# Two attention stages: weighing on GpSimd, the second head's copies on VectorE, scores as three f32r products

## The reference

```python
ss = jnp.einsum('qghd,gqkd->gqhk', qi, k_sel).astype(jnp.float32) * scale
smask = (k_pos <= t[None, :, None])[:, :, None, :]
p_s = jax.nn.softmax(jnp.where(smask, ss, NEG), axis=-1)
o_s = jnp.einsum('gqhk,gqkd->qghd', p_s.astype(dt), v_sel)
...
o = gi[..., 0:1] * o_c + gi[..., 1:2] * o_s + gi[..., 2:3] * o_w
```

## Time and profile before

| | us |
|---|---|
| median of 3 runs | 2058.59 |
| the profiled execution | 2057.08 |
| its span | 2055.2 |
| TensorE busy | 2026.5 |
| VectorE busy | 1181.4 |
| ScalarE busy | 796.5 |
| GpSimd busy | 27.0 |

### The profile page before, as it was taken

The page is one execution under the profiler, slowest core; times in us unless marked ns, Lnnn a source line. Parts: engine busy times, 40 slices in busy tenths (PEclk is TensorE's granted clock), DMA queues, the critical chain, the costliest instruction groups (busy, mean ns, idle before and its releaser), DMA issues.

```text
span 2055.2 us, 25553 instructions
## 1 busy us (share of the span) xinstructions
PE 2026.5 (99%) x9922; PEld 1647.7 (80%) x9922; DVE 1181.4 (57%) x1801; ACT 796.5 (39%) x1297; POOL 27.0 (1%) x58
## 2 busy tenths in 40 slices
PE   9999999999999999999999999999999999999998
PEld 8865878888888888877888888878886588888886
DVE  6777645454445356556565764764525857476475
ACT  4258242332212223245542432443324844243343
POOL 1000000000000000000000000000000000000000
PEclk9999999999999999999999999999999999999999
DMA  7310412322222222321323222231322132322222
GB/s 252 108 42 20 140 36 103 113 91 95 101 103 82 102 103 73 122 87 58 113 73 113 85 100 102 97 118 52 114 103 92 42 113 73 112 102 83 101 102 72
DMA packets 39425, 194.87 MB, mean 95 GB/s; under 512 B 4744, under 2 KB 13096, under 8 KB 19840
## 3 DMA queue, kind: packets, MB, share of 16 engines
q1 hardware_dynamic: 36240, 183.34, 25.3%
q0 software_dynamic: 2880, 9.88, 1.7%
q10 hardware_dynamic: 208, 0.33, 0.1%
HBM read 188.83 MB, written 2.15 MB: 93 GB/s over the span
## 4 chain that ended last, share of the span: by engine, by line
PE 93%; DVE 3%; ACT 2%; DVEq 1%; DMA 1%; issue 1%; SPq 0%; ACTq 0%
PE bank L443 26%; PE bank L444 26%; PE bank L445 26%; PE bank L1514 2%; PE bank L1501 2%; PE bank L1482 1%; PE bank L529 1%; PE bank L530 1%; PE bank L534 1%; DVE w_lo L391 1%; PE bank L2509 1%; ACT w_hi L372 1%; PE bank L2501 1%; PE bank L1707 0%; ACT work L1581 0%
## 5 line engine op out<-in xcount | busy, mean ns | idle before, releaser
L372 ACT ACTIVATE w_hi<-w_raw 128x2048 fp32r<-128x2048 f32 (+3 forms) x165 | 302.2, 1832 | 721.6 <-PE bank L445 679.0
L443 PE MATMUL bank<-a_hi,w_hi 128*128 128x512 f32 (+1 forms) x1408 | 540.6, 384 | 0.0
L445 PE MATMUL bank<-a_hi,w_lo 128*128 128x512 f32 (+1 forms) x1408 | 537.8, 382 | 0.0
L444 PE MATMUL bank<-a_lo,w_hi 128*128 128x512 f32 (+1 forms) x1408 | 537.8, 382 | 0.0
L391 DVE TENSOR_TENSOR w_lo<-w_raw,w_hi 128x2048 fp32r<-128x2048 f32 (+3 forms) x163 | 358.6, 2201 | 254.7 <-ACT w_hi L372 254.7
L445 PEld LDWEIGHTS bank<-a_hi,w_lo 128*128 128x128 f32 x1408 | 264.7, 188 | 51.7
L443 PEld LDWEIGHTS bank<-a_hi,w_hi 128*128 128x128 f32 x1408 | 264.8, 188 | 51.3 <-issue 0.8
L444 PEld LDWEIGHTS bank<-a_lo,w_hi 128*128 128x128 f32 x1408 | 264.8, 188 | 50.0
L443 PE MATMUL bank<-w_hi,big_halves 128*128 128x512 f32 x384 | 150.2, 391 | 0.3 <-DVE w_lo L391 0.3
L445 PE MATMUL bank<-w_hi,big_halves 128*128 128x512 f32 x384 | 149.5, 389 | 0.0
L444 PE MATMUL bank<-w_lo,big_halves 128*128 128x512 f32 x384 | 149.4, 389 | 0.0
(11 more groups left out here) (384 smaller groups left out, 2556.9 us busy)
## 6 DMA issues: line engine op xcount, KB each, us to landing
w_raw<-in_w_fu SPq DMA_DIRECT2D x44, 1024.0 KB, 4.8
w_raw<-in_w_up SPq DMA_DIRECT2D x16, 1024.0 KB, 4.8
w_raw<-in_w_down SPq DMA_DIRECT2D x16, 1024.0 KB, 4.8
w_raw<-in_w_fd SPq DMA_DIRECT2D x16, 1024.0 KB, 4.8
w_raw<-in_w_fd SPq DMA_DIRECT2D x8, 768.0 KB, 4.2
w_raw<-in_w_rqk SPq DMA_DIRECT2D x4, 1024.0 KB, 5.3
w_raw<-in_w_rvg SPq DMA_DIRECT2D x4, 1024.0 KB, 5.0
w_raw<-in_w_gate SPq DMA_DIRECT2D x4, 1024.0 KB, 4.8
```

Of the source, the lines that this page charges most:

```text
L372: act.activation(dst[0][:, cols], raw[slot][:, cols], ACT.Copy).then_inc(hi_half_ready.sem if half == 0 else hi_ready.sem, 1)
L443: pe.matmul(out, w[0], x[0], start=first, stop=False)
L444: pe.matmul(out, w[0], x[1], start=False, stop=False)
L445: return pe.matmul(out, w[1], x[0], start=False, stop=last)
```

## The change

GpSimd gets the tensor-scalars of `weigh`. VectorE keeps the reciprocal (`invert`) and gets the copies of the second head's turned tiles; ScalarE keeps the first head's. VectorE's step becomes maximum(s), invert(s-1), copy(s-3), take, and in the second attention `stage_low` for the next pair in steps of kind 0. TensorE waits for each head's copy on a semaphore of its own.

The scores become three f32r products. For this the queries and keys are staged as a high half (a ScalarE copy) and a low half (a VectorE subtraction). In the first attention six tiles are staged once, from the dense stage before, behind `outputs_copied` (L1816); in the second two tiles for each pair. The bias rows of the second attention are issued between GpSimd's weighings.

```diff
@@ tensor: score(u)
-                    if u == 0:
-                        pe.wait_ge(*ready)
+                    if u % G == 0:
+                        pe.wait_ge(staged.sem, b_st + staged_for(n))
...
-                    for i, w, at in members(u):
-                        for e in range(2):
-                            last = pe.matmul(out[e][:, at:at + w], q[heads[e], i * P:(i + 1) * P], k[heads[e], 0:w],
-                                             start=at == 0, stop=not causal and (i, at) == GROUPS[u % G][-1])
+                    for a, b in ((0, 0), (0, 1), (1, 0)):
+                        for i, w, at in members(u):
+                            for e in range(2):
+                                last = pe.matmul(out[e][:, at:at + w], q[a][heads[e], i * P:(i + 1) * P], k[b][heads[e], 0:w],
+                                                 start=a == 0 and b == 0 and at == 0,
+                                                 stop=not causal and a == 1 and (i, at) == GROUPS[u % G][-1])
@@ tensor: turn(u)
                     for e in range(2):
                         if u >= 1:
-                            pe.wait_ge(probs_copied.sem, b_c + 2 * u + e - 1)
+                            pe.wait_ge(copied[e][0], copied[e][1] + u)
@@ vector
+            def stage_low(dve, n):
+                for r, (st, src) in enumerate(stagings(n)):
+                    dve.wait_ge(high_staged.sem, b_hi + once + n * each + r + 1)
+                    dve.tensor_tensor(st[1], src, st[0].bitcast(F32), ALU.subtract).then_inc(staged.sem, 1)
...
-                def weigh(u):
-                    n, count = u // G, 2 * len(members(u))
+                def invert(u):
+                    count = 2 * len(members(u))
                     dve.wait_ge(probs_ready.sem, b_p + parts_until(u + 1))
-                    dve.reciprocal(row_sum[u % 3][:, 0:count], row_sum[u % 3][:, 0:count])
-                    dve.drain()
-                    for r, (i, w, at) in enumerate(members(u)):
-                        for e in range(2):
...
+                    dve.reciprocal(row_sum[u % 3][:, 0:count], row_sum[u % 3][:, 0:count]).then_inc(sums_inverted.sem, 1)
+
+                def copy(u):
+                    n, p = u // G, u // G % 2
+                    if n >= 2:
+                        dve.wait_ge(out_ready.sem, b_o + n - 1)
+                    dve.wait_ge(probs_turned.sem, b_t + 2 * u + 2)
+                    for i, w, at in members(u):
+                        if i == 3:
+                            dve.tensor_copy(turned_keys(p, 1, 3), turn_bank[1][:, 3 * P:4 * P])
+                        m = min(i + 1, 3)
+                        last = dve.tensor_copy(probs_t[p][1][:, 0:m, i * P:(i + 1) * P],
+                                               turn_bank[1][:, at:at + m * P].rearrange("p (j t) -> p j t", t=P))
+                    last.then_inc(second_copied.sem, 1)
@@ vector: step(s)
                     if unit(1) is not None:
-                        weigh(unit(1))
+                        invert(unit(1))
+                    if unit(LAG) is not None:
+                        copy(unit(LAG))
                     if last_of(unit(LAG + 2)):
                         take(unit(LAG + 2))
+                    if s % G == 0 and unit(0) is not None and s // G + 1 < pairs:
+                        stage_low(dve, s // G + 1)
@@ gpsimd
+                for u in range(groups):
+                    n = u // G
+                    pool.wait_ge(sums_inverted.sem, b_si + u + 1)
+                    for r, (i, w, at) in enumerate(members(u)):
+                        for e in range(2):
+                            x, scale = prob(u, e)[:, at:at + w], column(row_sum, u, r, e)
+                            if factor is None:
+                                ins = pool.tensor_scalar(x, x, scale, None, ALU.mult)
+                            else:
+                                ins = pool.tensor_scalar(x, x, scale, factor(n, e, i), ALU.mult, ALU.mult)
+                            ins.then_inc(weighted.sem, 1)
+                    if bias_next is not None and last_of(u) and n + 2 < pairs and n >= 1:
+                        bias_next(pool, n + 2)
@@ scalar
+            def stage_high(act, n):
+                if n == 1:
+                    act.wait_ge(evacuated.sem, b_e)
+                elif n >= 2:
+                    act.wait_ge(scores_ready.sem, b_s + G * (n - 1))
+                for st, src in stagings(n):
+                    act.activation(st[0], src, ACT.Copy).then_inc(high_staged.sem, 1)
...
-                    for e in range(2):
-                        act.wait_ge(probs_turned.sem, b_t + 2 * u + e + 1)
...
+                    act.wait_ge(probs_turned.sem, b_t + 2 * u + 1)
```

More of the change, by code:

```diff
@@ L237, in build @@
         with ExitStack() as same:
+            sb(same, "shared_probs", [P, 4352])
+            fx_first = sb(same, "fx_first", [P, 4, S], F32R)
+        with ExitStack() as same:
             sb(same, "shared_front", [P, 4096])
@@ L1427, in rotate, with attention @@
             return dve.tensor_tensor(x, x, swapped_x, ALU.add)
-        def attention(turns_n, q_of, k_of, v_of, ready, factor, finish, together, lent, probs, free, bias_of, bias_ready=None, causal=False, ends=None):
+        def attention(turns_n, q_of, k_of, v_of, static, space, factor, finish, together, lent, probs, free, bias_of, bias_ready=None, bias_next=None, causal=False, ends=None):
             GROUPS = (((0, 0), (1, P)), ((2, 0),), ((3, 0),))
@@ L1443, in attention, with staged_for, stagings @@
             score_bank, turn_bank, out_bank = bank[0:4], bank[4:6], (bank[7], bank[6])
-            b_s, b_m, b_p = scores_ready.n, max_ready.n, probs_ready.n
-            b_n, b_t, b_c, b_o, b_d = weighted.n, probs_turned.n, probs_copied.n, out_ready.n, out_done.n
+            b_st, b_s, b_m, b_p, b_hi = staged.n, scores_ready.n, max_ready.n, probs_ready.n, high_staged.n
+            b_n, b_t, b_o, b_d, b_si = weighted.n, probs_turned.n, out_ready.n, out_done.n, sums_inverted.n
+            copied = [(t.sem, t.n) for t in (first_copied, second_copied)]
             b_e, b_ro, b_cd = free
             heads = [slice(64 * e, 64 * e + 64) for e in range(2)]
+            held = [space(n) for n in range(pairs)]
+            once = len(static)
+            each = 0 if static else 2
+            def staged_for(n):
+                return once + each * (n + 1)
+            def stagings(n):
+                q, k = held[n]
+                return [] if static else [(q, q_of(n)), (k, k_of(n))]
             def members(u):
@@ L1505, in values @@
                     n, p = u // G, u // G % 2
-                    pe.wait_ge(probs_copied.sem, b_c + 2 * u + 2)
+                    for sem, before in copied:
+                        pe.wait_ge(sem, before + u + 1)
                     if n >= 2:
@@ L1603, in scalar @@
                 steps(LAG + 1, step)
+            staged.n += staged_for(pairs - 1)
+            high_staged.n += staged_for(pairs - 1)
             scores_ready.n += groups
@@ L1916, in first_projections, with nsa @@
             return stages + [attention_stage]
-        def nsa(o, vg, gate, ready, free):
+        def nsa(o, vg, gate, free):
             qk = big_tiles(0)
+            hold = big_tiles(1, dt=F32R)
+            keys = [[hold[:, 4 + p, :], hold[:, 6 + p, :]] for p in range(2)]
+            queries = [[hold[:, c, :], big_tiles(0, dt=F32R)[:, c, :]] for c in range(4)]
+            static = [(keys[p], qk[:, 6 + p, :]) for p in range(2)] + [(queries[c], qk[:, c, :]) for c in range(4)]
             def factor(n, e, i):
@@ L2984, in fox, with space @@
                         stages.append(dense("fg", two_chunks(a_tiles), none, none, none, gates_act, tile_ready=ready))
+                def space(n):
+                    if n == 0:
+                        return [[fx_first[:, r + h, :] for h in range(2)] for r in (0, 2)]
+                    return [[x[:, r + n % 2, :] for x in (a_hi, a_lo)] for r in (0, 2)]
                 def finish(dve, n, out):
@@ L3025, in begins @@
                     return lambda eng, b, slot, m: begin(eng) if b == 2 else None
-                stages.append(dense("fq", two_chunks(a_tiles), scaled_by(qT, float(FD) ** -0.5), none, none, begins(begin_high)))
-                stages += [attend, {"gpsimd": next_bias_rows}, {"scalar": split_high, "vector": lambda dve: split_low(dve, [KT - 1])}]
+                stages.append(dense("fq", two_chunks(a_tiles), scaled_by(qT, float(FD) ** -0.5), begins(begin_dve), none, begins(begin_high)))
+                stages += [attend, {"scalar": split_high, "vector": lambda dve: split_low(dve, [KT - 1])}]
                 split_hi_done.n += KT
@@ L3039, in build @@
         sigs = [work4[:, 0:2, :], work4[:, 2:4, :], region(5120, 2, S), region(5120 + 2 * S, 2, S)]
-        stages = first_projections(o, vg, gate, tables, lambda ready, free: nsa(o, vg, gate, ready, free))
```

(1 more changed line is left out.)

81 lines of the change are left out of this document (47 added, 34 removed).

## The result

The changed kernel takes 2088.24 us (median of 5 runs, 2087.18 to 2090.99); the kernel before took 2057.62 in the runs beside them (5 runs, 2056.51 to 2058.76). The medians are 30.6 us apart, where I had forecast about 16.5; the ratio is 1.0144, interval 1.0133 to 1.0155. The sign, the place and the first attention's period came out as argued; the second attention did not. The time lies at the very end of the range of 2064 to 2088, and well above the 2081 at which the forecast's own range ended.

The account below looks back on a forecast made before the run. TensorE, busy 99% of the span, was taken to bound the kernel. Added waits of 15.2 + 0.8 + 0.1 + 0.7 = 16.8 us on 2057.1 gave 2073.9, as a median 2075; range 2064 to 2088, the forecast's own 2069 to 2081.

Parts of the forecast that it names:

- The handshake, first attention: TensorE's second-head transposes wait for VectorE's copy, behind maxima and reciprocal: 9.10 us a pair, 1.34 more than 7.76.
- T1 to T2: From the end of kind 1's turn to the end of kind 2's: 2.46 us forecast, 2.08 before.
- T2 to T0: From the end of kind 2's turn to the end of kind 0's: 2.81 us forecast, 1.67 before.
- T0 to T1: From the end of kind 0's turn to kind 1's, first attention: TensorE decides, 3.83 us forecast, 3.95 before.
- The handshake, second attention: The same wait for VectorE's copy in the second attention: 9.19 us a pair against 7.99, 1.20 more.
- So I take it as hidden, near the floor: GpSimd's weighing, both attentions: near 0.9 ns per column, under the 3.9 that kind 0 allows, so no cost per pair.
- The fills: Starts of the attentions: 0.8 us for handshakes before the first full period, 0.1 first weighing, 0.7 second pair's staging.
- The scores: Three f32r products in both attentions: 0.52 us against 0.64 for 384 columns; only this 0.12 a pair counts.
- GpSimd bounds: Rival: above 3.9 ns per column GpSimd's own 10 us a pair set the pace over 14 pairs: 2089; chance 0.05.
- Staging collides: Rival, second attention: VectorE's low halves wait for GpSimd's wide tiles, next maxima 0.85 late seven times: 2081; chance 0.08.
- The f32r heads do not overlap: Rival, scores: six products run one behind the other, 0.75 us a pair over 14 pairs: 2086; chance 0.1.
- the wait is hidden: Rival, second head's transposes: VectorE's copy is ready in time and the scores' saving counts: 4.6 us off, 2054; chance 0.07.

## Why the prediction was right, and where it was not

- **The handshake, first attention: right.** T1 to T2 2.44 (2.46 forecast), T2 to T0 2.79 (2.81), T0 to T1 3.83 (3.83). Six periods cost 7.8 us, forecast 8.0, and moving the copy removes the gap. The chain was summed from the rows of before, all but two small terms: 0.05 to wake TensorE, and 0.25 for starting the transposes anew. No row shows these two by themselves; the gaps that they belong to came out shorter (0.30 and 0.74) and the intervals as summed.
- **The handshake, second attention: right but not what counts.** Once GpSimd is faster the period is 9.13 (9.19 forecast).
- **"So I take it as hidden, near the floor": the step that failed.** I had bounded the weighing at 0.9 to 3.6 ns per column, and took the memset's 0.9. It was 0.85 with two factors and 2.67 with one, within my bounds. The first is the floor; the second attention has the other form. Two things followed from that choice. I tested only the tightest deadline (3.9 ns per column for kind 0) and not GpSimd's whole pair: its eight tiles are 8.8 us, and the two issues of the bias's transfers, which GpSimd had all along, make it 9.84, over the handshake's 9.19. And I treated both attentions' weighing as one operation, though the diff shows two. The second attention lost 2.11 a pair instead of 1.20, 5.5 us more in six periods: 3.9 is GpSimd's 9.84 over the 9.19, and 1.6 the clock's.
- **The fills: mis-sized.** 0.8 + 0.1 + 0.7 = 1.6 forecast, 7.9 measured with the fourth turns and tails; the tails, which I had at nothing, are 1.3 of it, all in the second attention. In the second attention's first fill the chain of waits has these pieces:

```profile
1583.78 1.21 DVE a_lo L1550 x2
...
1586.14 0.60 POOL work L1622
...
1586.75 2.40 POOL work L1622 x3
...
1589.28 1.53 PE bank L1519 x6
```

The same work in the timeline of the kernel before:

```profile
1574.00 1.01 DVE L1550 TENSOR_SCALAR work<-work,row_sum 128x128 f32<-128x128 f32 x4
...
1575.15 0.84 PE L1501 MATMUL bank<-const_sb,work 128*128 128x128 f32 x6 [0.20 <-DVE work L1550]
```

GpSimd's first weighing takes 3.0 us where VectorE's took 1.01, the second pair's halves 1.21, and the turn, at half clock, 1.53 where it was 0.84. The first I had at 0.1, the second at 0.7, the third not at all.
- **The clock: not foreseen.** Every wait had been priced at its own length. In the second attention the values took up to 3.61 us instead of 2.30 where the clock was at half. It makes 2.3 us ahead of the first attention, in code that the change does not touch, and 1.6 in the second attention's six periods. What it adds to fills and tails is open. Waits of this kind do not bring a stretch each time: with the scores in f32 the first attention has the same intervals with a gap (2.44 and 2.79) and no stretch at all.
- **The scores: right.** 0.12 forecast between T0 and T1 and 0.12 measured, and 0.17 between T1 and T2 came as 0.16 where it shows. "For kind 0 I expect no gain" was kinder than the chip: 0.16 lost, under a wait in the changed kernel.
- **Staging ahead of the first attention: right,** hidden. In the profiles without the stretch at 96 us the first score starts at 131.56 to 131.92, against 131.85 before.
- **Rivals.** "GpSimd bounds" was the right mechanism, in one attention. I gave it 0.05 and a threshold of 3.9 ns per column; 2.67 was enough, since the transfers' issues belong to the same queue. Its 2089 is the nearest to the time measured by luck: it had both attentions at GpSimd's pace, and nothing for the longer fills and the clock. "Staging collides" (0.08) was right that there is a collision. I had VectorE waiting for both wide tiles and the next maxima 0.85 late; in the changed kernel it cost VectorE 0.21 us and GpSimd 0.16 a pair, 1.0 us in six periods. "The f32r heads do not overlap" fell with the scores' savings, and "the wait is hidden" with the gaps.

## What to carry to other kernels

Work that is given to another engine is to be summed over a whole period of that engine, with everything already in its queue and at the upper bound of its price; the tightest single deadline doesn't tell it. Where two places call the same helper with different operands, they are two instructions with two prices. And a copy that frees a bank for TensorE has no good place on an engine that also serves the next unit: behind the maxima it cost 0.98 us a pair in the first attention (9.06 against 8.08 with ScalarE's copies), ahead of them it moved the wait to the next engine.

## What the runs showed of the hardware

- GpSimd's tensor-scalar on f32 tiles in on-chip memory, in place: with one operation 600 ns for 128 columns and 1563 for 512 where VectorE does not disturb it, 2.5 ns per column; with two 449 and 775, 0.85 per column. Adding a multiplication by 1.0 saved 8.6 us of the whole kernel.
- VectorE's subtraction with two inputs in on-chip memory and GpSimd's tensor-scalar hold each other up, and most of it falls on the one that starts second. With the subtractions 0.18 us ahead, GpSimd's 512-column tile took 2.44 us for 1.56, and they lost nothing. With GpSimd 0.34 us ahead, the first subtraction took 0.89 us for 0.68 and GpSimd's second tile 1.73; in the form with two operations that second tile took 1.64 for 0.69.
- TensorE's granted clock went to 1.2 GHz for stretches of 3.4 us, or two or three of them on end. In the changed kernel one came after 0.44 us of work in 1.80, and one after 3.00 in 3.00. The second kind came in some profiles of the same code and not in others, and put the next stage back by 1.4 to 3.4 us.
